# The norm of the attention keys and queries between the z blocks, the splits of the merge inside the merge, and HGRN2's four output gate blocks in halves between the eight levels of its core

## What is computed

```
h = RMSNorm(x); z = h @ w_in                   # one projection, 42 blocks of 128 columns
q, k = rms_norm per head of 64 channels        # attention: z blocks 0-3 (q), 6 and 8 (two of the k)
o_a = sparse attention; o_d = gated DeltaNet
f = lb + (1-lb)*sigmoid(r_f); k = (1-lb)*sigmoid(-r_f)                  # HGRN2
A[t,s] = sum_c q[t,c] k[s,c] prod(f over s+1..t);  o_h = (q*F) S + A v
o_h = rms_norm(o_h) * sigmoid(r_og)            # r_og: z blocks 38-41, the output gate
x = x + (sum_i sigmoid(mg_i) * (o_i @ w_branch_i)) @ w_out
```

## Time and profile before

| | |
|---|---|
| time, median of 3 runs | 3315.14 us (3310.76 to 3319.74) |
| profiled execution, its own time | 3311.23 us |
| its span, first to last instruction | 3309.4 us |
| mean granted clock of TensorE | 0.944 of 2.4 GHz |
| PE busy | 3085.1 us, 93% of the span |
| DVE, ACT, POOL busy | 1117.9, 1108.2, 1138.1 us |

### The profile page before, as it was taken

How to read it: one execution, slowest core, us unless ns; L and a number is a source line. 1 busy time by engine, 2 the same in 40 slices (tenths; PEclk the granted TensorE clock), 3 DMA queues, 4 the chain that set the end, 5 groups by cost and what they waited for, 6 DMA issues and landing times.

```text
span 3309.4 us, 69905 instructions
## 1 busy us (share of the span) xinstructions
PE 3085.1 (93%) x29464; PEld 2661.0 (80%) x29464; DVE 1117.9 (34%) x2254; ACT 1108.2 (33%) x1935; POOL 1138.1 (34%) x664
## 2 busy tenths in 40 slices
PE   6999999987888998999999999998889699999998
PEld 5888888567877887888888888875778688878887
DVE  4222413634145336222232224146242434362210
ACT  4333332451223323433233323234412132243332
POOL 2444431423121333444434444134222123434344
PEclk9999997998897999999999999889888889999999
DMA  4333330100121232233333334111002312323333
GB/s 146 125 128 94 116 114 31 49 26 2 55 97 50 88 125 84 94 97 103 97 119 119 124 104 139 60 47 33 26 2 77 108 39 84 125 84 95 101 96 122
DMA packets 83569, 283.44 MB, mean 86 GB/s; under 512 B 13330, under 2 KB 22418, under 8 KB 80786
## 3 DMA queue, kind: packets, MB, share of 16 engines
q1 hardware_dynamic: 83202, 278.54, 26.1%
q10 hardware_dynamic: 144, 1.60, 0.1%
HBM read 265.01 MB, written 15.09 MB: 85 GB/s over the span
## 4 chain that ended last, share of the span: by engine, by line
PE 66%; issue 20%; POOL 6%; DVE 4%; ACT 1%; DVEq 1%; DMA 0%; POOLq 0%; ACTq 0%; SPq 0%
PE pair L2148 44%; POOL w_lo L2124 6%; PE pair L2175 4%; PE pair L386 1%; PE pair L2135 1%; PE pair L397 1%; PE pair L423 1%; PE pair L275 1%; PE pair L372 1%; PE pair L737 1%; PE pair L332 1%; PE pair L1065 1%; DVE h_lo L2656 1%; DVE arena L1386 1%; PE pair L125 1%
## 5 line engine op out<-in xcount | busy, mean ns | idle before, releaser
L2124 POOL TENSOR_TENSOR w_lo<-raw,w_hi 128x1024 f16<-128x1024 f32 x452 | 1001.8, 2227 | 1888.9 <-ACT w_hi L2120 1888.9
L2148 PE MATMUL pair<-h_hi,w_hi 128*128 128x260 f16 x4320 | 1196.7, 277 | 30.3 <-ACT arena L1804 28.0
L2148 PE MATMUL pair<-h_lo,w_hi 128*128 128x260 f16 x4320 | 1196.2, 277 | 0.0
L2148 PE MATMUL pair<-h_hi,w_lo 128*128 128x260 f16 x4320 | 1195.8, 277 | 0.0
L2148 PE MATMUL pair<-arena,w_hi 128*128 128x260 f16 x4096 | 688.1, 275 | 11.8 <-DVE arena L2759 11.8
L2120 ACT ACTIVATE w_hi<-raw 128x1024 f16<-128x1024 f32 x452 | 463.5, 1051 | 394.3 <-PE pair L2148 200.9
L2148 PE MATMUL pair<-arena,w_lo 128*128 128x260 f16 x2048 | 562.8, 275 | 0.0
L2148 PEld LDWEIGHTS pair<-h_hi,w_hi 128*128 128x128 f16 x4320 | 429.2, 99 | 92.3 <-issue 30.5
L2148 PEld LDWEIGHTS pair<-h_hi,w_lo 128*128 128x128 f16 x4320 | 427.0, 99 | 61.4
L2148 PEld LDWEIGHTS pair<-h_lo,w_hi 128*128 128x128 f16 x4320 | 427.0, 99 | 60.3
L2148 PEld LDWEIGHTS pair<-arena,w_hi 128*128 128x128 f16 x4096 | 400.6, 98 | 68.5 <-POOL w_lo L2124 9.0
(11 more groups left out here) (407 smaller groups left out, 3372.3 us busy)
## 6 DMA issues: line engine op xcount, KB each, us to landing
raw<-in_w_up SPq DMA_DIRECT2D x180, 512.0 KB, 3.6
raw<-in_w_z SPq DMA_DIRECT2D x84, 512.0 KB, 3.5
raw<-in_w_dn SPq DMA_DIRECT2D x64, 512.0 KB, 3.5
raw<-in_w_mg SPq DMA_DIRECT2D x48, 512.0 KB, 3.6
raw<-in_w_dn SPq DMA_DIRECT2D x32, 384.0 KB, 3.0
raw<-in_w_wb SPq DMA_DIRECT2D x24, 512.0 KB, 3.5
raw<-in_w_out SPq DMA_DIRECT2D x16, 512.0 KB, 3.5
arena<-in_slc_pages SPq DMA_DIRECT2D x32, 128.0 KB, 3.2
```

The lines of the kernel that those rows point to most:

```text
L2124: e.tensor_tensor(w_lo[s % 4], raw[s % 2], w_hi[s % 4], ALU.subtract).then_inc(w_split, 1)
L2148: mm = pe.matmul(out, w[s % 4][:, kw, :], xx(kx), start=(first and i == 0 and p == 0), stop=(last and i == len(ks) - 1 and p == 2))
```

## The change

Four things move, and nothing of the result is left out.

1. The norm of q and k is done between z blocks 3 and 9. The blocks come in the order `Z_ORDER`; the squares are made by ACT from PSUM beside the copy; the sums stand in 24 matmuls of 260 columns that address strips of 32 rows or columns of the array (`during_z`); the root and the reciprocal work on all 520 columns.
2. `merged` is split block by block inside the last eight steps of the merge.
3. `D.write_back` goes from SP's queue to ACT's, behind the copies of the rows of v; and the pieces of DeltaNet's end stand closer (two spread blocks behind each of blocks 32 and 33, three outer blocks behind 34 and 35, two behind 36).
4. The blocks 38 to 41 leave the loop of z blocks. Each half of one is put into a level of HGRN2's core.

```diff
+Z_ORDER = (0, 1, 2, 3, 6, 8, 4, 5, 7, 9)
+HALVED = (*range(10, 23), *range(38, 42))
...
+        def during_z(self, pe, l, slot):
+            def sums(squares, n):
+                for a in range(2):
+                    for c in range(n):
+                        mm = pe.matmul(pair[2][32 * c:32 * c + 32, a, 0:HALF], sums_of, squares[:, c, a * HALF:(a + 1) * HALF], ...)
+            if slot == 4:
+                s_("qq"); sums(sq4, 4).then_inc(*T_.step("qs"))
+            elif slot in (6, 7):
+                v_("qn0" if a else "qr")
+                for c in range(4):
+                    mm = pe.matmul(bank(4 + c)[:, 0:HALF], sel[r, :], rq[r, a * HALF:(a + 1) * HALF], ...)
+            elif slot == 8:
+                s_("kq"); v_("qn1"); sums(sqr, 2).then_inc(*T_.step("ks"))
+            elif slot == 9:
+                v_("kr")       # four matmuls, as for slots 6 and 7
...
@@ attention, tensor
-            norm_tensor(pe, l, m, T_, S_, V_, "n", 6, sqr, 2)
             pe.wait_ge(cmp_in, 16 * 2 * (l + 1))
             pe.wait_ge(padded, l + 1)
             s_("gates")
-            v_("nn5")
+            v_("kn")
@@ attention, scalar
+                a = e.activation(halves(dst), both(slot % 2), ACT.Copy)
+                if slot < 6:
+                    a = e.activation(halves(square), both(slot % 2), ACT.Square)
...
@@ DeltaNet, during_next
-            elif zi == 31:
+            elif zi == 30:
                 w(S_, "oqs")
-            elif 33 <= zi < 37:
-                spread_block(zi - 33)
-            elif 37 <= zi < 41:
-                outer(2 * (zi - 37))
-                outer(2 * (zi - 37) + 1)
+            elif 32 <= zi < 34:
+                spread_block(2 * (zi - 32))
+                spread_block(2 * (zi - 32) + 1)
+            elif 34 <= zi < 37:
+                for i in range(3 * (zi - 34), min(3 * (zi - 34) + 3, 8)):
+                    outer(i)
@@ HGRN2, tensor
             for i in range(8):
+                zi, a = 38 + i // 2, i % 2
                 for t in range(QT):
                     (near or far of level i, piece t)
-            w(S_, "vr")
+                    if i == 0 and t == 1:
+                        w(S_, "vr")
+                    if t == 1:
+                        m["z_half"](pe, l, zi, a, 0, 4)
+                m["z_half"](pe, l, zi, a, 4, KD)
+            pe.wait_ge(m["z_used"], ZT * l + 42)
@@ HGRN2, scalar
             a.then_inc(*S_.step("vr"))
+            D.write_back(e, l)
+            for h in range(6):
+                gate_half(h)              # sigmoid of a half; after every second one split_hi of a tile
             (am copies of level 5 and 6)
+            gate_half(6)
             (am copies of level 7)
+            gate_half(7)
@@ SP
-                    if s == 43:
-                        D.write_back(sp, l)
@@ merge, ACT (and DVE alike with merged_low)
+                        if i == 2 and b:
+                            merged_high(b - 1)
-                for b in range(KD):
-                    act_e.activation(merged_hi[:, b, :], merged[:, b, :], ACT.Copy).then_inc(merged_hi_done, 1)
+                merged_high(KD - 1)
```

More of the change, by code:

```diff
@@ L111, in nth @@
     return 16 * (i + 1) + order_of(i).index((k, a)) + 1
[L114 to L127, removed]
 def gate_tile(gate, t):
@@ L599, in vector @@
             a.then_inc(pages_moved, 1)
[L600 to L603, removed]
             e.tensor_scalar(qg, qscale, scalar_of("qg"), HD ** -0.5, ALU.mult, ALU.mult)
-            norm_vector(e, l, m, T_, S_, V_, "n", norm6, lambda i: qg[:, i:i + 1] if i < 4 else scalar_of("kg", i - 3),
-                        lambda i: None, 2)
+            s_("qd")
+            e.reciprocal(rq, rq).then_inc(*V_.step("qr"))
+            for a in range(2):
+                t_(f"qb{a}")
+                for c in range(4):
+                    qc = qT[:, c, a * HALF:(a + 1) * HALF]
+                    e.scalar_tensor_tensor(qc, qc, qg[:, c:c + 1], bank(4 + c)[:, 0:HALF], ALU.mult, ALU.mult)
+                e.drain().then_inc(*V_.step(f"qn{a}"))
+                e.wait_ge(m["z_used"], ZT * l + Z_ORDER.index(4 + a) + 1)
+                moved = e.tensor_copy(cmpT[:, a, :, 0:T // 16], of_16(kvT[:, a, 0:T]))
+            moved.then_inc(padded, 1)
+            s_("kd")
+            e.reciprocal(rk, rk).then_inc(*V_.step("kr"))
+            t_("kb")
+            for i in range(2):
+                kc = halves(kvT[:, 2 + 2 * i, :])
+                e.scalar_tensor_tensor(kc, kc, scalar_of("kg", i + 1), both(2 + i), ALU.mult, ALU.mult)
+            e.drain().then_inc(*V_.step("kn"))
             s_("ckstd")
@@ L1792, in w @@
                 e.wait_ge(steps.sem, steps.at(n, l))
-            for zi in range(26, 42):
+            for zi in range(26, 38):
                 e.wait_ge(m["z_ready"], ZT * l + zi + 1)
@@ L2607, in _ @@
             dve.wait_ge(loaded, 48)
+            for i in range(2):
+                dve.tensor_reduce(rowm[:, i:i + 1], ident[:, 16 * i:P:32], AX_X, ALU.add)
+            dve.drain()
+            for i in range(2):
+                dve.tensor_copy(sel[:, 64 * i:64 * i + 64], rowm[:, i:i + 1].to_broadcast([P, 64]))
             a0, a1 = lbl[:, 0:4], lbl[:, 4:8]
```

136 lines of the change are left out of this document (74 added, 62 removed).

## The result

The changed kernel takes 3260.57 us (median of 4 runs, 3258.39 to 3262.55). Its ratio to the kernel before is 0.9833, 95% interval 0.9816 to 0.9850. The gain of about 55 us has the forecast's sign, and the time lies in the stated range (3222 to 3276), but the forecast was a gain of 71. Between the two profiled executions the difference is 49.0 us (3311.23 and 3262.28), and the terms are compared on these two.

A forecast was written before the change was run, and what follows sets the result against it. PE, working nearly all the time, was taken as the bound, waiting for DVE in the core. 2 x (6.6 + 34.5 - 9.1 + 3.8) - 0.5 = 71 off 3311.2 gave 3240, plus 3.9: 3244 us, range 3222 to 3276.

The forecast's parts named there:

- A: Norm of q and k: sums moved between z blocks, less a new wait for the small gates; gains 6.6 us a layer.
- B: Loop of z blocks: four blocks and the 14.0 us wait leave, a 3.0 us wait comes; gains 34.5 a layer.
- C: HGRN2's core: takes in the block halves, 39.6 us instead of 30.5; costs 9.1 a layer (5 to 15).
- D: Merge's end: early splits let 18 matmuls run before the output projection's wait; gains 3.8 us a layer (2.7 to 7.2).
- rival 1: HGRN2's core: DVE stalls beside four POOL splits, up to 8.4 us a layer; 3261 us, chance 0.15.
- Rival 2: HGRN2's core: the clock stays at 1.2 GHz, core 65 us instead of 39.6; 3294 us, chance 0.12.
- rival 3: A weight tile is late again and the 14 us waits only move into the core; 3272 us, chance 0.07.
- Rival 4: Slower: halves never overlap DVE's chain at low clock, core some 78 us (point 75); 3333 us, chance 0.03.

The follow-up runs named there:

- e1: The changed kernel with the old norm of q and k behind block 9, the other three parts kept; 3276.23 us, ratio 0.9899 to the kernel before.
- e4: The kernel before with only the write of DeltaNet's states moved from SP's to ACT's queue; 3289.71 us, ratio 0.9936.
- e3: The changed kernel with all eight splits of the merged branches behind the merge again; 3260.93 us, ratio 0.9847 to the kernel before.
- e10: The changed kernel with small-gate sigmoid before weight splits, HGRN2's seven decay products later, and the merge's last high parts before ACT's weight splits; 3229.34 us.
- e5: The kernel before with 24 extra one-column matmuls at each of levels 0 to 5 of HGRN2's core; 3335.07 us, ratio 1.0054.
- e6: The changed kernel with only one eighth of POOL's low part made for the merge's first four tiles; 3264.38 us, ratio 0.9856 to the kernel before.
- e2: The changed kernel with blocks 38 to 41 whole in the loop of z blocks again; 3284.31 us, ratio 0.9927 to the kernel before.
- e11: e10 with DeltaNet's write issued before the copies of the rows of v, and the copy emptying bank 6 first; 3228.27 us.

## Why the prediction was right, and where it was not

**A** was right in its mechanism and nearly in size: 6.6 forecast, 8.5 in the trace (10.1 less the 1.6 of the compression), 8 to 11 by e1. The wait in front of the compression was forecast as 6.4 us ended by ACT, and is 6.5 and 6.7. The slow start of the compression was taken at 2.0 and cost 1.6 and 1.5 (26 records in its first 3.4 us at a granted clock of 0.52). The 24 matmuls, 12 of them sums and 12 spreads, were over-sized with 6 us: they take 4.75, of which 3.60 instead of 5 in front of block 9's end. Eight of them on four strips last 1.09 us, 0.14 each, and four on two strips 1.07, 0.27 each. So the earlier trace rows (two strips, 0.25 each) was the right row for two strips and not for four. The Trainium skill, page TensorEngine Tiling (Array Packing), section Theoretical Speedup, allows up to four times for strips of 32; the trace agrees as far as it goes, with half the time on twice the strips.

**B** had the right cause, which e4 shows: one DMA's wait on SP's queue held up tiles for which PE waited 14.0 us. The stretch gave 30.7 and 28.8 of the 34.5. The mis-sized term is the new wait at the outer blocks, 3.0 forecast and 6.6 measured. I had counted DVE's way to the third outer block once, and not the second group of three, which waits 2.6 for an addition that lasts 2.63 us beside a POOL split. Nor had I counted the slow start behind the wait of 4.0, although block 41 had shown one: the outer block and the z block behind it take 8.0 us (granted clock 0.79), those behind the wait of 2.6 take 6.3.

**C** is the step whose mechanism failed. Its sum had 5.8 for level 0, 4.5 for each of the levels 1 to 5, and 11.3 for the end; measured in the first layer are 5.8, five times 5.24, and 11.4. PE's own work is at most the 4.5 of the forecast (two times 0.76 and two times 1.50), so the 3.7 us are the stops of PE, five of 0.49 to 1.18 and 4.0 in all. In the second layer the levels 1 to 5 last as long, with stops of 2.56 and 0.40 and a granted clock of 0.66 in the 5 us behind the first of them. The failed sentence is "PE waits there for DVE": in the kernel before PE waited for code. The rows had it: the earlier trace rows say x126 where a level has 128 records, with "issue" as the releaser. The sum also put the price of the write in the core at nothing: with the write on ACT's queue the core lasts 33.4 us instead of 30.5 before any block is put into it (e4). ACT's queue was looked at for ACT's time, 2 us, and not for what the 2.5 MB do to other traffic. How much of the 3.7 us is the write's, no run shows. That 12.9 still lies in the stated 5 to 15 is luck: that range was not made for stops.

**D** was over-sized: 3.8 forecast (2.7 to 7.2), 1.6 measured from the same point of the merge to the next norm, and 0 to 2 by e3, within its interval nothing. The times of the last two splits came as forecast: PE goes on 4.2 and 6.7 us behind the point at which it stopped before, where k = 0 and 1 had come. What was wrong is the price of the 18 matmuls that now run in front of the wait, 0.21 each in the forecast of 3.8. They run at the full clock, 0.11, so 2.0 us are saved, and what is left behind the wait still starts slowly (granted clock 0.51). e10 shows what the part could give with its two splits out of ACT's way.

**Not in the sum** was the start of the merge. There HGRN2's 32 small matmuls (L1774) last 11.5 and 11.3 us instead of 9.1. This does not look like the work of the change: in the two layers of the other kernels they last anything from 9.0 to 11.9 us, also in e4 (9.3 and 11.1) and e5 (11.9 and 9.0), which have the old merge. The kernel before had the short case in both layers. What decides between the cases is not shown. By size alone, the stretch of the merge (5.5 and 5.1 us a layer below its forecast) and B (3.8 and 5.7) missed as much as C (3.8 and 3.5).

**The rivals.** The measured time is to the microsecond that of rival 1, 3261, and its stalls are in the trace, 1.98 and 2.21 us for 0.42. By the Trainium skill, page SBUF — State Buffer, section Who interferes with whom, a DVE instruction with two SBUF inputs contends with a GpSimd instruction that reads SBUF; the trace agrees, and in e6 the same operation lasts 0.50 us at most. But e6 takes the stalls away and gains nothing. A time that fits a rival is no evidence for it. Rival 2 is refuted by the core's granted clock of 1.00 and 0.96, rival 3 by e2 and by the waits. Rival 4 stays far off, with a core of 43 us where it needed 75.

**What stays open** is what sets the 3.3 to 6 us between two packets of code. They came further apart where 2 MB passed by DMA (6.0 us once in e4, at a DMA share of 0.92), and about 4 apart where little did (e5, at 0.06). That the write delays the code is thus likely, but no run here changes the packets alone.

## What to carry to other kernels

Count the instructions of a stretch of many short matmuls, and look whether PE stops after equal numbers of them, inside a run without a wait. If so, suspect its code. Here neither a faster partner (e6) nor a shorter wait (e11) helped then, while added instructions (e5) and a DMA put there (e4) cost time. When a DMA that blocks a queue is moved to another engine, price where its bytes will pass, too. When a wait is hidden by work that is taken away, look at what stood in front of the step that it waits for: here two weight splits had no reason to be there, and moving them, with the table loaded early, gave 14 us by the medians and 17 by the ratios, nearly as much as the norm itself (16 and 22).

## What the runs showed of the hardware that I had not expected

In the levels 0 to 5 of HGRN2's core PE stopped 126 or 127 matmul records behind the stop before, or a multiple of that (126 are some 256 instructions, an estimate), and went on 2.0 to 2.8 us after the start of a 16 KB packet of the queue "instruction"; these packets began 3.3 to 6 us apart. In the loops of the feed-forward no such packet came: from 100 to 200 us of the kernel before the view has none. A write of 2.5 MB during the core made it 3 us longer with the same work on every engine (33.4 instead of 30.5).
